# Strassen block products for 20 of 22 up-projection tiles in a two-layer decoder trunk

## What is computed

```
def conv_ffn(h, w_up, conv_w, conv_b, w_down):      # h: 512 x 1024, w_up: 1024 x 5632
    gate, val = jnp.split(h @ w_up, 2, axis=-1)      # two halves of 2816 channels
    gate = causal depthwise convolution of width 3 over the tokens, plus conv_b
    return (jax.nn.silu(gate) * val) @ w_down        # w_down: 2816 x 1024
```

## Time and profile before

| what | value |
|---|---|
| median of 3 runs | 1221.37 us (1221.35 to 1221.38) |
| span of the profiled execution | 1219.5 us |
| PE busy | 1207.9 us, 99% of the span |
| DVE / ACT / POOL busy | 507.8 / 501.6 / 567.4 us |
| channel products (L1600) on the chain that ended last | 38% of the span |
| mean traffic to and from memory | 93 GB/s |

### The profile page before, as it was taken

The page is one execution under the profiler, slowest core; times in us unless marked ns, Lnnn a source line. Parts: engine busy times, 40 slices in busy tenths (PEclk is TensorE's granted clock), DMA queues, the critical chain, the costliest instruction groups (busy, mean ns, idle before and its releaser), DMA issues.

```text
span 1219.5 us, 16989 instructions
## 1 busy us (share of the span) xinstructions
PE 1207.9 (99%) x6230; PEld 1036.3 (85%) x6230; DVE 507.8 (42%) x900; ACT 501.6 (41%) x743; POOL 567.4 (47%) x509
## 2 busy tenths in 40 slices
PE   8999999999999999999999999999999999999997
PEld 7999999888888888888888889888888888888886
DVE  7878777653211212323241375635321212232325
ACT  6665555544322223423342366344332322343234
POOL 2435544335444444566645332613544444456662
PEclk9999999999999999999999999999999999999999
DMA  7222222113222222222223211301322222222221
GB/s 270 92 98 95 79 70 70 67 38 121 103 103 103 73 99 103 104 84 89 104 87 121 87 70 57 117 36 39 123 98 103 103 92 86 97 103 104 75 98 70
DMA packets 17325, 113.71 MB, mean 93 GB/s; under 512 B 1920, under 2 KB 2304, under 8 KB 4608
## 3 DMA queue, kind: packets, MB, share of 16 engines
q1 hardware_dynamic: 16416, 110.20, 25.2%
q10 hardware_dynamic: 864, 2.88, 0.7%
HBM read 110.98 MB, written 2.10 MB: 93 GB/s over the span
## 4 chain that ended last, share of the span: by engine, by line
PE 95%; DVE 2%; ACT 1%; issue 1%; DMA 0%; DVEq 0%; SPq 0%; ACTq 0%
PE ps L1600 38%; PE ps L1893 16%; PE ps L1681 9%; PE ps L1543 7%; PE ps L1572 3%; PE ps L2024 2%; PE ps L1722 2%; PE ps L1645 2%; PE ps L2004 2%; PE ps L1590 2%; PE ps L1650 1%; PE ps L1928 1%; PE ps L1708 1%; PE ps L1491 1%; PE ps L1734 1%
## 5 line engine op out<-in xcount | busy, mean ns | idle before, releaser
L316 POOL TENSOR_TENSOR w_lo<-w_raw,w_hi 128x512 fp32r<-128x512 f32 (+1 forms) x329 | 462.5, 1437 | 515.5 <-ACT w_hi L413 459.5
L413 ACT ACTIVATE w_hi<-w_raw 128x2048 fp32r<-128x2048 f32 (+1 forms) x93 | 171.9, 1848 | 309.1 <-PE ps L1600 155.2
L1600 PE MATMUL ps<-hT_hi,w_hi 128*128 128x512 f32 x688 | 267.7, 389 | 0.0
L1600 PE MATMUL ps<-hT_hi,w_lo 128*128 128x512 f32 x688 | 267.7, 389 | 0.0
L1600 PE MATMUL ps<-hT_lo,w_hi 128*128 128x512 f32 x688 | 267.6, 389 | 0.0
L1600 PEld LDWEIGHTS ps<-hT_hi,w_hi 128*128 128x128 f32 x688 | 129.1, 188 | 26.8
L1600 PEld LDWEIGHTS ps<-hT_lo,w_hi 128*128 128x128 f32 x688 | 129.1, 188 | 26.8
L1600 PEld LDWEIGHTS ps<-hT_hi,w_lo 128*128 128x128 f32 x688 | 129.1, 188 | 26.7
L1235 DVE TENSOR_TENSOR hT_lo<-region,hT_hi 128x2048 fp32r<-128x2048 f32 (+1 forms) x22 | 58.9, 2684 | 144.0 <-ACT hT_hi L686 144.0
L1205 DVE SCALAR_TENSOR_TENSOR qk<-ps,vec,qk 128x511 f32<-128x511 f32 x44 | 33.0, 750 | 200.1 <-ACT qk L660 200.1
L660 ACT ACTIVATE qk<-ps,vec 128x512 f32<-128x512 f32 x44 | 34.3, 780 | 175.5 <-PE ps L1600 166.3
(11 more groups left out here) (278 smaller groups left out, 2102.3 us busy)
## 6 DMA issues: line engine op xcount, KB each, us to landing
w_raw<-weights SPq DMA_DIRECT2D x99, 1024.0 KB, 4.8
gain<-gains ACTq DMA_DIRECT2D x4, 512.0 KB, 3.5
x<-x_in SPq DMA_DIRECT2D x3, 512.0 KB, 7.5
out<-region SPq DMA_DIRECT2D x3, 512.0 KB, 2.7
w_raw<-weights SPq DMA_DIRECT2D x2, 384.0 KB, 5.6
w_raw<-weights SPq DMA_DIRECT2D x1, 768.0 KB, 8.6
cst<-consts SPq DMA_DIRECT2D x1, 640.0 KB, 10.2
x<-x_in ACTq DMA_DIRECT2D x1, 512.0 KB, 4.1
```

The lines of the kernel that those rows point to most:

```text
L316: ins = pool.tensor_tensor(w_lo[:, slot, cols], w_raw[:, slot, cols], w_hi[:, slot, cols].bitcast(f32), ALU.subtract)
L413: sc.activation(w_hi[:, slot, 0:used], w_raw[:, slot, 0:used], ACT.Copy).then_inc(w_hi_ready, 1)
L1600: ins = pe.matmul(bank, w[:, slot, k * pitch + 128 * s:k * pitch + 128 * s + 128], h[:, k:k + 1, :], start=k == 0 and n == 0, stop=k == KT ...
```

## The change

In each layer, pair 0 (the first gate and value tile) is computed as before. The other 20 tiles are computed by Strassen's scheme (in Winograd's form) on 2 by 2 blocks. A block of weights A is 512 features by 128 channels, a block of activations B is 512 features by 256 tokens; A11, A12, A21, A22 and four sums S1 to S4 meet B11, B21, B22 and four sums T1 to T4 in seven products P1 to P7. Each product has 4 blocks by 3 passes with 256 moving columns, 12 matmuls; a tile has 84.

- The host orders the weight tiles by blocks (`blocks`).
- T1 to T4 are made once for a layer, at the start of the MLP: ACT copies six of the eight transposed blocks from PSUM to SBUF (`copy_raw`), DVE makes the sums and ACT, DVE and POOL split them. T3 overwrites B12 in `hT_hi` and `hT_lo`, after the first value tile.
- For each block tile ACT copies A21 to a PSUM bank (`stage_a21`), and DVE makes S1 and S2 in PSUM and S3 and S4 in SBUF (`block_sums`); ACT makes the high parts (`block_high` for 1536 columns, `sum_highs` for the sums, where S2 is read twice), DVE the low part of S1 (`first_low`), POOL the low parts of A11, A12, A22, S2, S3 and S4: six pieces of 512 columns.
- A gate tile uses banks 0 to 3, a value tile 4 to 7. P1 is copied to SBUF by ACT (`copy_p1`), and DVE combines the products in place in five operations (`combine_block`): three of 256 columns and two of 512, with three `own.link` waits. Products that are added last, P4 with P3, share a bank.
- The convolution, SiLU and multiplication are as before, but the SiLU is taken in place.
- PE runs pairs 2 to 9 in the loop, pairs 1 and 10 outside of it. The last tile takes its products in the order 1, 7, 2, 5, 6, 4, 3, so that a part of `hT_hi` and `hT_lo` is free early for the first activations of the down-projection; `first_hi` and `first_lo` are gone.
- The load of `gain` moves from the start of the MLP to its end, because its memory holds sums.

The diff, cut to its core. On POOL:

```
+            def block_lows(l, n0):
...
+                with pool.Fori(1, PAIRS) as i:
+                    for half in range(2):
+                        tile = 2 * i + (half - 2)
+                        pool.wait_ge(w_hi_ready, 2 * i + (n0 + half + 1))
+                        for a in (0, 512):
+                            low(w_lo[:, half, a:a + 512], w_raw[:, half, a:a + 512], w_hi[:, half, a:a + 512])
+                        pool.wait_ge(s_summed[l], tile + 1)
+                        low(w_lo[:, half, 1024:1536], w_raw[:, half, 1024:1536], w_hi[:, half, 1024:1536])\
+                          .then_inc(w_lo_ready, 1)
+                        for a, highs in ((0, 3), (512, 4), (1024, 4)):
+                            pool.wait_ge(s_high[l], 4 * tile + highs)
+                            low(s_lo[half][:, a:a + 512], s_raw[half][:, a:a + 512], s_hi[half][:, a:a + 512])\
+                              .then_inc(s_low[l], 1)
...
```

On ACT:

```
+                def pair(i, first=False, last=False):
+                    stage_a21(i, 1)
+                    block_high(i, 1)
+                    copy_p1(i, 0)
+                    sum_highs(i, 1)
+                    if last:
+                        split_after(n1 - 2)
+                    else:
+                        stage_a21(i + 1, 0)
+                        block_high(i + 1, 0)
+                    copy_p1(i, 1)
+                    sc.wait_ge(combined[l], 2 * i - 1)
+                    for s in range(2):
+                        gate_start(i, s, ps[:, s, :])
+                    if not last:
+                        sum_highs(i + 1, 0)
+                    silu(i)
+                    if last:
+                        first_highs()
...
```

On DVE:

```
+                def block_sums(i, half):
...
+                    own.link(ve.tensor_tensor(s1, s1, a22, ALU.add))
...
+                    ins = ve.tensor_tensor(s2, s1, a11, ALU.subtract)
+                    ins.then_inc(s1_ready[l], 1)
+                    ve.wait_ge(s1_ready[l], 2 * i + (half - 1))
+                    ve.wait_ge(mm_done, 8 * i + 4 * (n0 + half - 1))
+                    ve.tensor_tensor(s_raw[half][:, 512:1024], a22, s2, ALU.subtract)
+                    ve.tensor_tensor(s_raw[half][:, 1024:1536], a12, s2, ALU.subtract).then_inc(s_summed[l], 1)
...
+                def pair(i, last=False):
+                    block_sums(i, 1)
+                    first_low(i, 1)
+                    combine_block(i, 0)
+                    if not last:
+                        block_sums(i + 1, 0)
+                    convolve(i, (ps[:, 0, :], ps[:, 1, :]))
+                    if not last:
+                        first_low(i + 1, 0)
+                    else:
+                        first_lows()
+                    combine_block(i, 1)
+                    multiply(i)
```

On PE:

```
+                PARTS = {1: ("A11", "B11", 3, 0), 2: ("A12", "B21", 0, 0), 3: ("S4", "B22", 2, 0),
+                         4: ("A22", "T4", 2, 256), 5: ("S1", "T1", 1, 0), 6: ("S2", "T2", 0, 256), 7: ("S3", "T3", 1, 256)}
...
+                def product(half, p):                                # PE
+                    left, right, bank, col = PARTS[p]
+                    (wh, wl), (th, tl) = weights_of(half, left), moving(right)
+                    for k in range(4):
+                        for n, (w, t) in enumerate(((wh, th), (wh, tl), (wl, th))):
+                            ins = pe.matmul(ps[:, 4 * half + bank, col:col + 256], w[:, 128 * k:128 * k + 128], t[:, k, :],
+                                            start=k == 0 and n == 0, stop=k == 3 and n == 2)
...
+                def block_tile(i, half, first=False, last=False):
...
+                    if half:
+                        pe.wait_ge(act_done[l], 2 * i)
+                    else:
+                        pe.wait_ge(conv_done[l], 2 * i)
+                    pe.wait_ge(w_lo_ready, 2 * i + (n0 + half + 1))
+                    pe.wait_ge(s1_low[l], 2 * i + (half - 1))
+                    product(half, 1).then_inc(product_done[l], 1)
+                    for p in (7, 2, 5, 6, 4, 3) if last else (2, 5, 6, 4, 7, 3):
+                        if p in (6, 7, 3):
+                            pe.wait_ge(s_low[l], 6 * i + 3 * (half - 2) + {6: 1, 7: 2, 3: 3}[p])
...
+                with pe.Fori(2, LAST) as i:
+                    block_tile(i, 0)
+                    block_tile(i, 1)
```

More of the change, by code:

```diff
@@ L26 @@
 LO_COLS = 512
+REGION = 17024
+PAIRS = FT // 2
+LAST = PAIRS - 1
 IN_COLS = 4 * 384
@@ L654, in mlp, with gate_start @@
                 n1 = n0 + FT
[L656 to L663, removed]
+                def gate_start(i, s, source):
+                    col = V_CONV + l * FT * 4 + 4 * s
+                    sc.activation(qk[:, s, :], source, ACT.Identity, scale=vec[:, ds(8 * i + (col + 2), 1)],
+                                  bias=vec[:, ds(8 * i + (col + 3), 1)]).then_inc(conv_started[l], 1)
@@ new lines, in mlp @@
+                for j, summed in enumerate((1, 3, 4)):
+                    sc.wait_ge(t_summed[l], summed)
+                    sc.activation(t_hi[j][:, :, :], t_raw[j][:, :, :], ACT.Copy).then_inc(t_high[l], 1)
+                stage_a21(1, 0, start=True)
+                for s in range(2):
+                    sc.wait_ge(mm_done, 4 * n0 + 2 * s + 2)
+                    gate_start(0, s, ps[:, 6 + s, :])
+                block_high(1, 0)
+                silu(0)
+                sum_highs(1, 0)
@@ L680, in mlp @@
+                sc.wait_ge(t_summed[l], 4)
+                sc.wait_ge(mm_done, 4 * (n0 + 2))
+                sc.activation(hT_hi[:, 0:4, 256:512], t3_raw, ACT.Copy).then_inc(t_high[l], 1)
+                pair(1, first=True)
+                with sc.Fori(2, LAST) as i:
                     pair(i)
-                pair(FT // 2 - 1, first_highs)
+                pair(LAST, last=True)
                 def halves(u0, kt, slot, count=4):
@@ L1227, in mlp @@
+                ve.wait_ge(t_high[l], 4)
+                ve.tensor_tensor(hT_lo[:, 0:4, 256:512], t3_raw, hT_hi[:, 0:4, 256:512].bitcast(f32), ALU.subtract)\
+                  .then_inc(t43_low[l], 1)
+                with ve.Fori(1, LAST) as i:
+                    end = own.loop(i - 1, LAST - 1, 10)
                     pair(i)
                     end()
-                pair(FT // 2 - 1, first_lows)
+                pair(LAST, last=True)
                 def lows_of(done, u0, kt, slot, count=4):
@@ L1549, in final_norm, with first_tile @@
                 return norms[0] == 4
-            def first_tile(tile):
-                slot = tile % 2
+            def first_tile(tile, l=None):
+                slot, blocked, bank = tile % 2, l is not None, 0 if l is None else 6
                 pe.wait_ge(w_hi_ready, tile + 1)
@@ L1874, in mlp, with weights_of @@
-                pair(0, first=True)
-                with pe.Fori(1, FT // 2) as i:
-                    pair(i)
-                n1 = n0 + FT
-                def down_tile(slot, parts, last, wait_w, wait_lo, beside=False):
+                n1 = n0 + FT
+                def weights_of(half, name):
+                    if name in ("A11", "A12", "A22", "S1"):
+                        j = ("A11", "A12", "A22", "S1").index(name)
+                        return tuple(w[:, half, 512 * j:512 * j + 512] for w in (w_hi, w_lo))
+                    j = ("S2", "S3", "S4").index(name)
+                    return tuple(w[half][:, 512 * j:512 * j + 512] for w in (s_hi, s_lo))
@@ new lines, in mlp @@
+                first_tile(n0, l)
+                pe.wait_ge(w_lo_ready, n0 + 2)
+                pe.wait_ge(t_summed[l], 3)
+                for s in range(2):
+                    channels(1, s, ps[:, 4 + s:5 + s, :], True)
+                block_tile(1, 0, first=True)
+                block_tile(1, 1)
+                with pe.Fori(2, LAST) as i:
+                    block_tile(i, 0)
+                    block_tile(i, 1)
+                block_tile(LAST, 0)
+                block_tile(LAST, 1, last=True)
@@ L1881, in down_tile @@
+                def down_tile(slot, parts, last, wait_w, wait_lo):
                     pe.wait_ge(w_lo_ready, wait_w)
@@ L1900, in mlp @@
                 every, four = (1, 1, 1, 1), (0, 1, 2, 3)
-                down_tile(0, [(0, four, True, False, every)], False, n1 + 1, 4, beside=True)
+                pe.wait_ge(conv_done[l], 2 * PAIRS)
+                down_tile(0, [(0, four, True, False, every)], False, n1 + 1, 4)
+                pe.wait_ge(act_done[l], 2 * PAIRS)
                 with pe.Fori(0, 2) as i:
```

262 lines of the change are left out of this document (196 added, 66 removed).

## The result

The changed kernel takes **1188.18 us** (median of 4 runs, 1188.03 to 1188.40); the kernel before took 1221.36 beside it. The ratio is 0.9729, with a 95% interval of 0.9715 to 0.9743: 33.2 us less. The forecast was 1197 us, with a range from 1192 to 1213. So it is faster, as forecast, but by 8.7 us more than I said, and outside the range on the good side. The profiled execution spans 1186.2 us, 33.3 less than before.

The account below looks back on a forecast made before the run. PE bounds the kernel, the others delivering in time. Its gain of -32.1 us plus 2 x (2.5 + 1.3) us for the MLPs' starts and ends gives -24.5 us from 1221.37: forecast 1197 us, range 1192 to 1213.

Parts of the forecast that it names:

- The bound and PE's gain: Block tiles: PE sets the time; 84 matmuls of 120.0 ns replace 48 of 226.7 ns, saving 0.80 us a tile.
- fixed part: PE matmuls: each pays 13.3 ns beyond its columns at 2.4 GHz, at 256 and 512 columns alike.
- term -32.1: PE's gain over 40 block tiles: 10.88 us a tile before, 10.08 after, so -32.1 us.
- Durations of the others: Loop: PSUM-writing DVE operations 0.69 us for 512 columns, POOL pieces 1.26, A21 on ACT 0.59; DVE busy near 85%.
- The order of waits in the loop: Each pair: the last wait, S1's low part, is met 1.9 us early, so PE never waits; cost 0.
- The start of each MLP, +2.5 a layer: First block tile: POOL's third piece at 299.3 plus 0.5 for register waits makes it 2.5 us late, between 0 and 5.
- The end of each MLP, +1.3 a layer: First down tile: split activations ready at 11.1 to 12.5 us, due at 10.08, so +1.3 us (1.0 to 2.5).
- DVE as a small bound: Rival, loop: DVE needs 20.4 to 21.4 us a pair and bounds the kernel, 1202 to 1222 us; chance 0.10.
- PE's bookkeeping: Rival, loop: PE's register waits and branch cost 0.74 us a pair, +12 us, 1209 us; chance 0.05.
- a shrinking fixed part: Rival, block tiles: without 13.3 ns for each matmul, DVE bounds a tile near 9.5 us, 1174 us; chance 0.02.
- dear PSUM writes: Rival, loop: DVE operations writing PSUM take 1.23 us instead of 0.69, +82 us, 1279 us; chance 0.11.

Follow-up runs that it names:

- before_256: The kernel before, with each channel product of 512 columns made as two of 256, same sums: 1249.36 us, ratio 1.0228.
- swap_places: The changed kernel with the SBUF places of the sums S2 to S4 exchanged between gate and value tile: 1188.44 us, ratio 0.9730.
- dve2: The changed kernel with two DVE memsets of 1024 columns, each waited for, ahead of the convolution in pairs 1 to 9: 1199.99 us, ratio 0.9826.
- dve4: The changed kernel with four DVE memsets of 1024 columns, each waited for, ahead of the convolution in pairs 1 to 9: 1269.33 us, ratio 1.0397.
- head1: The changed kernel with one waited-for DVE memset of 1024 columns ahead of T4 at the start of each MLP: 1196.11 us, ratio 0.9787.
- head_late: The changed kernel with one waited-for DVE memset of 1024 columns ahead of the convolution of pair 0: 1190.69 us, ratio 0.9749.
- all_sbuf: The changed kernel with S1 and S2 in SBUF, no A21 copy, S1's low part ahead of the convolution: 1219.26 us, ratio 0.9983.
- tail_plain: The changed kernel with each layer's last tile taking its products in the common order 1, 2, 5, 6, 4, 7, 3: 1194.48 us, ratio 0.9779.

## Why the prediction was right, and where not

- **The bound and PE's gain**: right. PE at its own pace, 84 matmuls a tile, 13.3 ns of fixed part (13.5 by before_256). The term -32.1 should have been 40 x (10.88 - 10.03) = -33.9, since a matmul costs 119.46 ns. This is 1.8 us of the miss, mis-sized; its cause is open, and swap_places shows only that the short products move with the place of the sums.
- **Durations of the others**: right. PSUM writes 0.69 to 0.70 (taken: 0.69), POOL 1.27 to 1.30 (1.26), A21 0.60 (0.59). DVE is busy 15.4 us of 20.05 a pair, 77% where I had written near 85%. One reading was thinner than I made it: the four POOL pieces of the earlier trace rows end at 500.30, and the DVE operation at 499.52 stands beside the last 0.8 us of them, not in their middle. The rows of the kernel after now show POOL's pace beside such operations.
- **The order of waits in the loop**: right. Cover 2.1 us, forecast 1.9; 2.1 also gives the waits of dve2 (0.5) and dve4 (2.9) from their delays (2.6 and 5.0).
- **The start of each MLP, +2.5 a layer**: the step that failed. I had the third piece at 299.3 and 0.5 more for register waits; it ended at 297.19. T1 to T3 ended 0.6 us earlier (285.66 for 286.3). From there to the end of T4's low part it took 4.6 us where I had 5.2: T4 took 1.22, not 1.93, since it starts at 285.69, just ahead of POOL at 285.74, while its low part, beside POOL, took 2.22. No working of mine had that order of 0.05 us (it is the same in the second layer), so it was luck, and head1 shows the other case. The convolution and the sums took 0.4 less each. The 0.5 for register waits wasn't there. 5.0 us of the miss.
- **The end of each MLP, +1.3 a layer**: failed too. My own working gave 11.1 - 10.08 = 1.0; the 0.3 above it has no source. (The 1.9 for the down weights isn't 1.49 x 2048 / 1536 either, which is 2.0; it measured 1.92.) The low parts end 10.0 us after the tile before (488.1 to 498.07), not 11.1, and PE waits 0.13. By the end of the convolution, 5.9 us in where I had 6.8, 0.9 of that is there. Some 0.3 is its links, which cost 0.15 in the loop and about 0.03 outside of it, where the wait is for a constant (290.19 + 0.74 to 290.96). The other 0.6 lies ahead of it, where ACT's three operations overlap by 0.1 us each time. 2.3 us of the miss.
- **The sum**: 1.8 + 5.0 + 2.3 = 9.1, against 8.7; the down-projections, 0.26 longer each, take back 0.5. In the range I had let the end cost nothing, but the start at least 1 us, though I had written "between 0 and 5" for it; with 120.0 ns that is 1191.3, which I wrote as 1192. With 0 it would have been 1189.3, still above the measured 1188.18, because of the 1.8 us of the matmuls.
- **The rivals**: DVE as a small bound (a pair of 20.05 us, no wait), PE's bookkeeping (a pair takes 20.05 us in the loop and 20.15 outside of it), a shrinking fixed part (before_256) and dear PSUM writes (0.69) are all refuted. The last would have been dear indeed: dve4, with 5 us more on DVE in a pair, is slower than before. The place of the danger was right, but it was the operands in SBUF that carry it, not the writes to PSUM.

## What to carry to other kernels

When PE is the bound and the others are to deliver more, count the cover at the last wait of a period and then ask of each elementwise operation how many operands it reads from SBUF while POOL works: that choice alone was worth 30 us here. Durations from inside a loop don't hold outside of it: take links and register waits for each stage from a row of that stage, and where two engines start within 0.1 us of each other, work out which comes first, since the second pays: T4 took 1.22 us or 2.46 by that. A margin of 0.2 us at a stage's start is worth nothing to build on: 1.3 us of work there cost 1.2 us a layer.

## What the runs showed of the hardware

- **Some waits of PE cost more than their length.** Waits of 0.53 (dve2), 1.2 (head_late) and 2.2 us (all_sbuf) left the granted clock at 1.00. Behind waits of 2.5 us in the first layer it was 0.65 and 0.79 (tail_plain), or 0.63 and 0.80 (head1), in the next two windows of 3 us: half clock, then full. The length of the wait alone doesn't decide: head1's second layer shows half clock again, tail_plain's second layer, behind the same 2.5 us, doesn't, and in dve4 it follows 14 of 18 waits of 2.9 us. Some 26 of dve4's 81 us are the clock. What decides between two equal waits is open.
- **DVE and POOL hold each other up only where DVE reads two operands from SBUF**: 0.69 to 1.78 us for 512 columns, 1.22 to 2.46 for 1024, and POOL's two pieces of 512 2.55 to 3.45. In head1 POOL started first and took 2.41 us, and DVE's T4 took 2.46 instead of 1.22.
- **With the place of the sums in SBUF a matmul of 256 columns moves by up to 2%** (P3: 1.412 or 1.440 us for its twelve); the cause is open, and the place isn't all of it.
